# Second feed-forward product: other positions for two row pairs, and weight-block differences made by negated copies and accumulating transfers

## The chip, the cores and the metric

The kernel runs on one core of a Trainium2 chip. The metric is the device time of one execution in microseconds. A core has TensorE (matmuls, from weights loaded into its array and a moving operand), VectorE, ScalarE, GpSimd and SyncE, which here only issues transfers. The engines run side by side and wait for each other by counting semaphores; each works through its own instructions in order.

## The reference, cut to what matters

One layer of a streaming encoder on 256 tokens of width 2048, in float32: a gated convolution and latent attention, a cross attention to 256 memory rows, and a feed-forward of width 8192, which the change is about.

```
def squared_relu_mlp(h, w1, w2):
    return jnp.square(jax.nn.relu(h @ w1)) @ w2
...
x = x + squared_relu_mlp(rms_norm(x, norm_ffn_g[l]), w_ff1[l], w_ff2[l])
```

## The kernel before, in words

**Products in three parts.** A float32 product is made of three matmuls: each factor is split into a high and a low part, and high x high, high x low and low x high are added up (`product`, L2022). The splits of the activations are made once. Those of the weights are made as they stream in: SyncE loads a unit of 128 x 1024 values (two row blocks of 128, each 512 columns wide, 512 KB) into one of four slots of `raw` (`load`, L417); ScalarE copies it to the high part (`hi`, L619); VectorE subtracts that from the raw value for the low part (`lo`, L1075); TensorE uses both. SyncE issues the load of a unit once VectorE has split the unit four before it. ScalarE splits a unit once TensorE has finished the unit four before it. Both run LEAD = 3 units ahead in program order: at step k of a stage ScalarE and VectorE handle unit k + 3.

**The feed-forward.** It is done in four groups (g) of 2048 hidden columns. A group has 32 units of the first product (`still_unit`), and then two half-passes of the second product, p = 0 and 1 (here called pairs of column chunks, or pairs), each 16 units (`seven_pair`, L2027), for output columns 1024p to 1024p + 1023, that is, two chunks c = 0 and 1 of 512. Sixteen row blocks k of the weight times two token blocks t times two chunks are multiplied. For row blocks 0 to 3 the kernel doesn't use the ordinary eight block products of a 2 x 2 by 2 x 2 block matrix but seven (Strassen's scheme in Winograd's form): with A the hidden activations and W the weight, differences and sums of blocks are multiplied. There are two such sides, m = 0 (row blocks 0 and 1) and m = 1 (row blocks 2 and 3).

**Units of a pair.** `FF2_ORDER` lists (c, k) in the order of the units. Twelve are full: two row blocks x two token blocks x three matmuls, 12 matmuls. The unit (0, 2m) is the *left* one of side m, with 6 matmuls, and (1, 2m) the *right* one, with 3; they stand next to each other, at 7 and 8 for m = 0 and at 11 and 12 for m = 1. After the unit at 13 and after the one at 14 come 12 matmuls each on the weight differences of both sides, the tail. That makes 186 matmuls per pair.

**The differences.** While both units of side m stand in `raw`, VectorE's `w_sums` (L1392) makes four differences of their 128 x 512 blocks: t1 = right's first minus left's first and t3 = right's second minus right's first, in one instruction of 1024 elements; t2 = right's second minus t1; t4 = left's second minus t2. It stands ahead of VectorE's split of the left unit, since the slot is loaded anew after that. ScalarE's `ws_high` (L854, steps 5 and 10) copies them to their high parts, VectorE's `ws_low` (L1409, steps 5, 6 and 10, 11) makes the low parts, 1024 elements at a time. Of a right unit only the second half is split for TensorE (`hi_second` L626, `lo_second` L1081).

**The order** on each engine is written out by hand: ScalarE's in its `ff_group` (y_out, then the split of unit k + 3, then ws_high at a step), VectorE's in its own (w_sums, then the split, then ws_low, then the additions of results to the residual), SyncE's in `ff_loads` (L484). GpSimd does nothing in the feed-forward until the last gain vector is loaded. The last pair (g = 3, p = 1) has an order of its own, `LAST_ORDER`, and the output projections and the convolution's (which also use `seven_pair`) keep `FF2_ORDER`.

## Time and profile before

| | us |
|---|---|
| median of 3 runs | 1606.09 (1605.94 to 1606.55) |
| span of the profiled execution, first to last instruction | 1604.8 |
| TensorE busy | 1595.9 (99%) |
| VectorE busy | 1252.5 (78%) |
| ScalarE busy | 866.1 (54%) |
| GpSimd busy | 75.9 (5%) |
| DMA, share of 16 engines, hardware queue | 58.9% |

The profile gives no time of its own for the profiled execution beside the span; the median of the runs stands 1.3 us above it. A matmul's record is longer than the distance to the next one, because they are pipelined: the pace is read from the starts, not from the durations. Engines: PE is TensorE, PEld its weight load, DVE VectorE, ACT ScalarE, POOL GpSimd, SP SyncE; a q behind a name is its issuing side.

### The profile page before, as it was taken

The page shows a single profiled execution, that of the slowest core. Times are in us where ns is not written, and L with a number is a line of the kernel's source. Part 1 is how long each engine was busy: PE and PEld are TensorE (multiplying, and loading weights), DVE is VectorE, ACT ScalarE, POOL GpSimd, SP SyncE. Part 2 cuts the span into 40 slices and gives each one's busy share as a digit, 9 for nine tenths or more (in the row PEclk, how much of TensorE's full clock was granted, in tenths as well). Part 3 has the DMA queues.
Part 4 walks back from the last instruction along what each step waited for, and adds up shares of the span by engine and source line. Part 5 has one row for each costly group of instructions (what it writes and reads, how often), then busy time and mean ns, then how long its engine had stood idle before and what let it go on. Part 6 is the DMA issues. An engine that isn't in the chain of part 4 may idle for free.

```text
span 1604.8 us, 22691 instructions
## 1 busy us (share of the span) xinstructions
PE 1595.9 (99%) x7962; PEld 1352.9 (84%) x7962; DVE 1252.5 (78%) x1681; ACT 866.1 (54%) x1120; POOL 75.9 (5%) x160
## 2 busy tenths in 40 slices
PE   9999999999999999999999999999999999999998
PEld 8888888888888888888888888888888888888886
DVE  5588889999989898786887665885677666866587
ACT  7444456555555556754566655454464455545555
POOL 6500010000000000000000000000000000000001
PEclk9999999999999999999999999999999999999999
DMA  7665645555555665556664566666666666666555
GB/s 256 203 192 184 196 151 171 177 176 174 184 171 170 210 207 181 200 183 238 210 197 138 164 186 191 201 198 190 190 211 196 182 185 196 197 197 187 192 187 182
DMA packets 161294, 304.97 MB, mean 190 GB/s; under 512 B 11689, under 2 KB 20513, under 8 KB 160801
## 3 DMA queue, kind: packets, MB, share of 16 engines
q1 hardware_dynamic: 160128, 300.45, 58.9%
q0 software_dynamic: 1056, 3.46, 0.6%
q8 instruction: 51, 0.84, 0.2%
q14 instruction: 27, 0.22, 0.0%
q10 hardware_dynamic: 32, 0.01, 0.0%
HBM read 301.78 MB, written 2.10 MB: 189 GB/s over the span
## 4 chain that ended last, share of the span: by engine, by line
PE 98%; DVE 1%; DMA 1%; issue 0%; ACT 0%; SPq 0%; ACTq 0%; POOL 0%; DVEq 0%; POOLq 0%
PE ps L2255 15%; PE ps L1750 12%; PE ps L1752 12%; PE ps L1751 12%; PE ps L2025 9%; PE ps L2024 9%; PE ps L2023 9%; PE ps L2257 7%; PE ps L1763 1%; PE ps L1929 1%; PE ps L2146 1%; PE ps L1932 1%; PE ps L1914 1%; PE ps L1913 1%; PE ps L1912 1%; DMA raw<-in_w_ff_dram 1%
## 5 line engine op out<-in xcount | busy, mean ns | idle before, releaser
L1079 DVE TENSOR_TENSOR w_both<-raw,w_both 128x1024 fp32r<-128x1024 f32 x538 | 656.6, 1223 | 257.0 <-ACT w_both L624 255.3
L624 ACT ACTIVATE w_both<-raw 128x1024 fp32r<-128x1024 f32 x538 | 568.7, 1060 | 527.7 <-PE ps L1752 181.7
L2255 PE MATMUL ps<-a_both,w_both 128*128 128x512 f32 x1024 | 321.9, 396 | 0.0
L1750 PE MATMUL ps<-w_both,a_both 128*128 128x512 f32 x636 | 252.4, 397 | 0.1
L1752 PE MATMUL ps<-w_both,a_both 128*128 128x512 f32 x636 | 248.3, 390 | 0.0
L1751 PE MATMUL ps<-w_both,a_both 128*128 128x512 f32 x636 | 248.2, 390 | 0.0
L2257 PEld LDWEIGHTS ps<-a_both,w_both 128*128 128x128 f32 x1024 | 192.5, 188 | 45.2
L1140 DVE SCALAR_TENSOR_TENSOR acc<-hconv,cwk,acc 128x256 f32<-128x256 f32 x464 | 205.1, 497 | 7.4 <-PE ps L1968 7.4
L2257 PE MATMUL ps<-a_both,w_both 128*128 128x256 f32 x1024 | 201.4, 278 | 0.0
L2023 PE MATMUL ps<-w_both,c_hi 128*128 128x512 f32 x504 | 196.7, 390 | 0.3 <-DVE w_both L1079 0.3
L2025 PE MATMUL ps<-w_both,c_lo 128*128 128x512 f32 x504 | 196.4, 390 | 0.0
L2024 PE MATMUL ps<-w_both,c_hi 128*128 128x512 f32 x504 | 196.3, 390 | 0.0
L2255 PEld LDWEIGHTS ps<-a_both,w_both 128*128 128x128 f32 x1024 | 156.3, 189 | 0.3
L1752 PEld LDWEIGHTS ps<-w_both,a_both 128*128 128x128 f32 x636 | 119.5, 188 | 25.1
L1750 PEld LDWEIGHTS ps<-w_both,a_both 128*128 128x128 f32 x636 | 119.6, 188 | 23.8 <-issue 0.3
L1751 PEld LDWEIGHTS ps<-w_both,a_both 128*128 128x128 f32 x636 | 119.7, 188 | 23.3
L2023 PEld LDWEIGHTS ps<-w_both,c_hi 128*128 128x128 f32 x504 | 94.7, 188 | 20.2 <-DVE w_both L1079 0.8
L2025 PEld LDWEIGHTS ps<-w_both,c_lo 128*128 128x128 f32 x504 | 94.7, 188 | 19.4
L2024 PEld LDWEIGHTS ps<-w_both,c_hi 128*128 128x128 f32 x504 | 94.7, 188 | 19.4
L1750 PE MATMUL ps<-w_both,c_hi 128*128 128x512 f32 x128 | 50.2, 392 | 0.0
L1752 PE MATMUL ps<-w_both,c_lo 128*128 128x512 f32 x128 | 49.9, 390 | 0.0
L1751 PE MATMUL ps<-w_both,c_hi 128*128 128x512 f32 x128 | 49.9, 390 | 0.0
(377 smaller groups left out, 1920.3 us busy)
## 6 DMA issues: line engine op xcount, KB each, us to landing
raw<-in_w_ff_dram SPq DMA_DIRECT2D x256, 512.0 KB, 4.1
raw<-in_w_in_dram SPq DMA_DIRECT2D x144, 512.0 KB, 3.6
raw<-in_w_mla_out_dram SPq DMA_DIRECT2D x32, 512.0 KB, 3.7
raw<-in_w_conv_out_dram SPq DMA_DIRECT2D x32, 512.0 KB, 4.3
raw<-in_w_out_dram SPq DMA_DIRECT2D x32, 512.0 KB, 4.5
raw<-in_w_ukv_dram SPq DMA_DIRECT2D x16, 512.0 KB, 3.8
raw<-in_w_xkv_dram SPq DMA_DIRECT2D x16, 512.0 KB, 4.0
raw<-in_w_uq_dram SPq DMA_DIRECT2D x16, 384.0 KB, 3.3
```

The costliest lines, as they stand in the source:

```text
L624: act.activation(whi[:, s, :], raw[:, s, :], ACT.Copy).then_inc(hi_ready, 1)
L1079: dve.tensor_tensor(wlo[:, s, :], raw[:, s, :], whi[:, s, :].bitcast(F32), ALU.subtract).then_inc(lo_ready, 1)
L1140: ins = dve.scalar_tensor_tensor(out=to, in0=h[:, tap:tap + SEQ], scalar=cwk[:, tap:tap + 1], in1=to, op0=ALU.mult, op1=ALU.add)
L1750: pe.matmul(sum_, x_hi[:, k0 + k, tok], w_hi, start=(first and k == 0), stop=False)
L1751: pe.matmul(sum_, x_hi[:, k0 + k, tok], w_lo, start=False, stop=False)
L1752: mm = pe.matmul(sum_, x_lo[:, k0 + k, tok], w_hi, start=False, stop=(last and k == kts - 1))
L1763: tr = pe.transpose(ps[:, first + b, SEQ * (k % 2) + P * t:SEQ * (k % 2) + P * (t + 1)], src[:, t, c0 + P * k:c0 + P * (k + 1)], ident[:])
L2023: pe.matmul(ps[:, bank, :], x_hi, w_hi, start=first, stop=False, skip_group_check=True)
L2024: pe.matmul(ps[:, bank, :], x_hi, w_lo, start=False, stop=False, skip_group_check=True)
L2025: return pe.matmul(ps[:, bank, :], x_lo, w_hi, start=False, stop=last, skip_group_check=True)
L2255: pe.matmul(both, whi[:, s, cols[n]], a_both[:, :, k0 + k, :], start=(first and k == 0), stop=False)
L2257: mm = pe.matmul(ps[:, b0 + b + n, 0:SEQ], wlo[:, s, cols[n]], a_hi[:, k0 + k, :], start=False, stop=(last and k == 1))
```

## The change

In seven of the eight pairs (all but the last):

- the order of the units is `FF_ORDER`: left and right units stand at 6 and 7 (m = 0) and at 9 and 10 (m = 1). The tail stays after the units at 13 and 14.
- `w_sums` is not called. Instead ScalarE's `negated` writes minus the first block of the left unit (step 3 for m = 0, step 6 for m = 1) and minus the first block of the right unit (steps 4 and 7) to the two halves of a buffer t13, ahead of its split of that unit. GpSimd then issues one accumulating transfer, which adds the right unit's two blocks from HBM to t13: that gives t1 and t3.
- SyncE loads the second blocks of the right and the left unit to a buffer t24, by two transfers of 256 KB, behind the loads of units 4 (m = 0) and 7 (m = 1).
- VectorE's `t_sums`, ahead of its splits at steps 6 (m = 0) and 9 (m = 1), waits for both and subtracts twice on 512 elements: t2 and t4, in place.
- ScalarE's `ts_high` (steps 6 and 10) and VectorE's `ts_low` (steps 6, 7 and 10, 11) do for t13 and t24 what `ws_high` and `ws_low` did for `w_sum`.

Context is cut to a line around each edit; a line "..." marks what is left out.

```diff
@@ -140,6 +140,10 @@
 LAST_LEFT, LAST_RIGHT = (3, 8), (4, 9)
+FF_ORDER = ((0, 4), (0, 6), (1, 4), (1, 6), (0, 8), (1, 8), (0, 0), (1, 0), (0, 10), (0, 2),
+            (1, 2), (1, 10), (0, 12), (0, 14), (1, 12), (1, 14))
+FF_LEFT, FF_RIGHT = (6, 9), (7, 10)
+TAIL = 13
 OUT = -1
...
 SEVENS = 2 * GROUPS + 3
@@ -163,6 +167,11 @@
+
+def made_before(g, p):
+
+    return 6 * (p + 1) if g is OUT else g * 8 + (4 * p + 18)
 def turn_pieces(n):
@@ -278,6 +287,8 @@
         ws_lo = ((ws_a0_lo, ws_b0_lo), (ws_a1_lo, ws_b1_lo))
+        t13 = (at(o - nbytes([P, TT, 2 * D]) + 8192, "t13_0", [P, 2 * NC]), at(o + 12288, "t13_1", [P, 2 * NC]))
+        t24 = (at(o - nbytes([P, TT, 2 * D]) + 12288, "t24_0", [P, 2 * NC]), at(o + 2048, "t24_1", [P, 2 * NC]))
         late = Sevens(w_sum, ws_hi, ws_lo, h_sum, h_hi, h_lo, y_copy)
...
         cs_m = [at(o + at_byte, f"cs_m{n}", [P, 2 * NC], F32R) for n, at_byte in enumerate((8192, 12288, 24576, 28672))]
@@ -390,6 +401,8 @@
         ones_copied, ones_added = sem("ones_copied"), sem("ones_added")
+        t24_landed, t13_added = [sem("t24_landed0"), sem("t24_landed1")], [sem("t13_added0"), sem("t13_added1")]
+        t_negated = sem("t_negated")
         fin_act, fin_dve, stored = sem("fin_act"), sem("fin_dve"), sem("stored")
         xq_bank = (2 * pair_of(N_XQ), 4)
@@ -485,9 +498,14 @@
                 for p in range(2):
-                    for i, (c, k) in enumerate(LAST_ORDER if last and p else FF2_ORDER):
+                    for i, (c, k) in enumerate(LAST_ORDER if last and p else FF_ORDER):
                         n = 2 * p + c
                         load(U_FF + UPC * CH + FF2_UNITS * p + i, r, w_ff2[:, ds(g * KT + k, 2), NC * n:NC * (n + 1)])
+                        if i in (4, 7) and not (last and p):
+                            m = (4, 7).index(i)
+                            sp.wait_ge(ws_lo_ready, g * 8 + (4 * p + 12))
+                            sp.dma_start(t24[m][:, 0:NC], w_ff2[:, g * KT + (2 * m + 1), NC * (2 * p + 1):NC * (2 * p + 2)]).then_inc(t24_landed[m], 16)
+                            sp.dma_start(t24[m][:, NC:], w_ff2[:, g * KT + (2 * m + 1), NC * (2 * p):NC * (2 * p + 1)]).then_inc(t24_landed[m], 16)
...
                 ff_loads(g, g * FF_UNITS, False)
@@ -602,6 +620,14 @@
+
+            for n in range(2 * GROUPS - 1):
+                g, p = n // 2, n % 2
+                for m in range(2):
+                    k = g * KT + 2 * m
+                    pool.wait_ge(t_negated, 4 * n + 2 * m + 2)
+                    pool.dma_start(t13[m][:].rearrange("p (k n) -> p k n", k=2), w_ff2[:, k:k + 2, NC * (2 * p + 1):NC * (2 * p + 2)],
+                                   accum_op=ALU.add).then_inc(t13_added[m], 16)
...
             pool.dma_start(fin_g[:], final_norm_g.rearrange("(o n) -> o n", o=1).to_broadcast([P, D])).then_inc(fin_landed, 16)
@@ -853,9 +879,22 @@
-                act.wait_ge(ws_made, g * 12 + (6 * p + 3 * (m + 1) + 18))
+                act.wait_ge(ws_made, made_before(g, p) + 3 * (m + 1))
                 for half in (1, 0):
...
+
+            def negated(g, p, m, u, n, r):
+
+                act.wait_ge(ws_lo_ready, g * 8 + (4 * p + 12))
+                s = u % RING
+                act.wait_ge(landed[s], 16 * (u // RING + 1) + r * (16 // RING))
+                act.activation(t13[m][:, NC * n:NC * (n + 1)], raw[:, s, 0:NC], ACT.Copy, scale=-1.0).then_inc(t_negated, 1)
+
+            def ts_high(g, p, m):
+
+                act.wait_ge(ws_made, g * 8 + (4 * p + 2 * m + 20))
+                for half, t in ((1, t24), (0, t13)):
+                    act.activation(late.ws_hi[m][half][:], t[m][:], ACT.Copy).then_inc(ws_hi_ready, 1)
...
@@ -1024,11 +1063,18 @@
                     ends = last and p == 1
-                    right, sums = (LAST_RIGHT, (1, 7)) if ends else (RIGHT, (5, 10))
+                    right, sums = (LAST_RIGHT, (1, 7)) if ends else (FF_RIGHT, (6, 10))
+                    tail = LAST_LEFT[1] + 2 if ends else TAIL
                     for k in range(FF2_UNITS):
                         n = UPC * CH + FF2_UNITS * p + k + LEAD
-                        if k == right[1]:
+                        if k == tail - 1:
                             y_out(g, p, 0)
+                        if not ends:
+                            for m in range(2):
+                                if k + LEAD == FF_LEFT[m]:
+                                    negated(g, p, m, U_FF + n, 0, r)
+                                if k + LEAD == FF_RIGHT[m]:
+                                    negated(g, p, m, U_FF + n, 1, r)
                         if k + LEAD in right:
...
                         elif not last or n < FF_UNITS:
@@ -1037,9 +1083,11 @@
                             ff_high(CH - 1, g * CH + CH)
-                        if k in sums:
+                        if k in sums and ends:
                             ws_high(g, p, sums.index(k))
-                        if k == right[1] + 2:
+                        elif k in sums:
+                            ts_high(g, p, sums.index(k))
+                        if k == tail + 1:
                             y_out(g, p, 1)
...
                             act.wait_ge(chunk_out, N_END - CH + 2)
@@ -1391,7 +1439,7 @@
-                done = 6 * p + 3 * m + 18
+                done = made_before(g, p) + 3 * m
                 u += left_at[m]
...
                 for n in range(2):
@@ -1401,10 +1449,25 @@
                                   ALU.subtract).then_inc(ws_made, 1)
-                dve.wait_ge(ws_made, g * 12 + (done + 1))
+                dve.wait_ge(ws_made, done + 1)
                 dve.tensor_tensor(t2, right[:, NC:], t1, ALU.subtract).then_inc(ws_made, 1)
-                dve.wait_ge(ws_made, g * 12 + (done + 2))
+                dve.wait_ge(ws_made, done + 2)
                 dve.tensor_tensor(t4, left[:, NC:], t2, ALU.subtract).then_inc(ws_made, 1)
+
+            def t_sums(g, p, m):
+
+                done = g * 8 + (4 * p + 2 * m + 18)
+                dve.wait_ge(t13_added[m], g * 32 + (16 * p + 16))
+                dve.wait_ge(t24_landed[m], g * 64 + (32 * p + 32))
+                dve.tensor_tensor(t24[m][:, 0:NC], t24[m][:, 0:NC], t13[m][:, 0:NC], ALU.subtract).then_inc(ws_made, 1)
+                dve.wait_ge(ws_made, done + 1)
+                dve.tensor_tensor(t24[m][:, NC:], t24[m][:, NC:], t24[m][:, 0:NC], ALU.subtract).then_inc(ws_made, 1)
+
+            def ts_low(g, p, m, half):
+
+                dve.wait_ge(ws_hi_ready, g * 8 + (4 * p + 2 * m + 2 - half + 12))
+                dve.tensor_tensor(late.ws_lo[m][half][:], (t13, t24)[half][m][:], late.ws_hi[m][half][:].bitcast(F32),
+                                  ALU.subtract).then_inc(ws_lo_ready, 1)
...
@@ -1671,14 +1734,17 @@
                     ends = last and p == 1
-                    left, right, lows = (LAST_LEFT, LAST_RIGHT, ((1, 2), (7, 8))) if ends else (LEFT, RIGHT, ((5, 6), (10, 11)))
+                    left, right, lows = (LAST_LEFT, LAST_RIGHT, ((1, 2), (7, 8))) if ends else (FF_LEFT, FF_RIGHT, ((6, 7), (10, 11)))
+                    tail = LAST_LEFT[1] + 2 if ends else TAIL
                     u = UPC * CH + FF2_UNITS * p
...
                         i = k + LEAD
-                        if i in left:
+                        if i in left and ends:
                             w_sums(g, p, left.index(i), U_FF + u, r, left)
+                        if not ends and k in (6, 9):
+                            t_sums(g, p, (6, 9).index(k))
                         if i in right:
...
                         elif not last or u + i < FF_UNITS:
@@ -1689,11 +1755,11 @@
                             if k in lows[m]:
-                                ws_low(g, p, m, 1 - lows[m].index(k))
-                        if k == right[1] + 2:
+                                (ws_low if ends else ts_low)(g, p, m, 1 - lows[m].index(k))
+                        if k == tail + 1:
                             dve.wait_ge(p4_done, g * 2 + (p + 4))
                             add_chunk(p, 0)
-                        if k == right[1] + 3:
+                        if k == tail + 2:
                             add_copies(g, p, g * CH + (N_FF + 2 * p + 1))
...
                             add_last(g, p)
@@ -2024,7 +2090,7 @@
-            def seven_pair(g, p, u, r, banks, first_use, between, sums, b=late, x_hi=c_hi, x_lo=c_lo, order=FF2_ORDER, left=LEFT, right=RIGHT):
+            def seven_pair(g, p, u, r, banks, first_use, between, sums, b=late, x_hi=c_hi, x_lo=c_lo, order=FF2_ORDER, left=LEFT, right=RIGHT, tail=TAIL):
...
                     tok = slice(P * t, P * (t + 1))
@@ -2062,11 +2128,11 @@
                             for t in range(TT):
-                                ends = n == 1 and (i == 15 or (i == left[1] + 2 and t == 0))
+                                ends = n == 1 and (i == 15 or (i == tail and t == 0))
                                 mm = product(banks[c] + t, *hidden(k + n, t), *slot(i, n), first=banks[c] + t not in begun, last=ends)
...
                         mm.then_inc(used, 1)
-                    if i == left[1] + 2:
+                    if i == tail:
                         pe.wait_ge(ws_lo_ready, g * 8 + (4 * p + 15))
...
                         for m in range(2):
@@ -2075,7 +2141,7 @@
                         mm.then_inc(p4_done, 1)
-                    if i == left[1] + 3:
+                    if i == tail + 1:
                         pe.wait_ge(ws_lo_ready, g * 8 + (4 * p + 16))
...
                         for m in range(2):
@@ -2283,18 +2349,19 @@
                     pe.wait_ge(ff_lo, g * CH + (k // 4 + 1))
-                    if i == LEFT[0]:
+                    if i == FF_LEFT[0]:
                         pe.wait_ge(ff_sum, g * CH + CH)
...
-                    if i == (LAST_LEFT if last else LEFT)[0]:
+                    if i == (LAST_LEFT if last else FF_LEFT)[0]:
                         pe.wait_ge(mixed, g * 6 + 12)
                 u = U_FF + UPC * CH
-                seven_pair(g, 0, u, r, FF2_BANKS[0], ff_waits, lambda i: None, g + 3)
+                plain = dict(order=FF_ORDER, left=FF_LEFT, right=FF_RIGHT)
+                seven_pair(g, 0, u, r, FF2_BANKS[0], ff_waits, lambda i: None, g + 3, **plain)
                 pe.wait_ge(chunk_out, g * CH + (N_FF + 1))
-                seven_pair(g, 1, u + FF2_UNITS, r, FF2_BANKS[1], mixed_waits, lambda i: None, g + 3, **dict(order=LAST_ORDER, left=LAST_LEFT, right=LAST_RIGHT) if last else {})
+                seven_pair(g, 1, u + FF2_UNITS, r, FF2_BANKS[1], mixed_waits, lambda i: None, g + 3, **dict(order=LAST_ORDER, left=LAST_LEFT, right=LAST_RIGHT, tail=LAST_LEFT[1] + 2) if last else plain)
...
             for g in range(1, GROUPS - 1):
```

## Rows read from the trace of the kernel before

**Rows 1.** The page: parts 1 to 3, whole execution.
```profile
span 1604.8 us, 22691 instructions
...
PE 1595.9 (99%) x7962; PEld 1352.9 (84%) x7962; DVE 1252.5 (78%) x1681; ACT 866.1 (54%) x1120; POOL 75.9 (5%) x160
...
PEclk9999999999999999999999999999999999999999
...
q1 hardware_dynamic: 160128, 300.45, 58.9%
q0 software_dynamic: 1056, 3.46, 0.6%
```
**Rows 2.** The page, part 4: the chain that ended last, by engine.
```profile
PE 98%; DVE 1%; DMA 1%; issue 0%; ACT 0%; SPq 0%; ACTq 0%; POOL 0%; DVEq 0%; POOLq 0%
```
**Rows 3.** Waits of TensorE: total us, times, longest us.
```profile
PE ps L1779 <- POOL stat L517: 1.5, 1, 1.5
PE ps L2023 <- DVE w_both L1079: 0.3, 1, 0.3
```
**Rows 4.** Windows on the second product's stretches, one per group: busy us by engine.
```profile
992.30:1076.60 84.30, 84.30 (x374) 69.88 (x373) 68.21 (x65) 44.24 (x47) 0.00 (x0) 1.00 0.64 205
...
1339.30:1424.30 85.00, 84.67 (x375) 69.81 (x374) 68.56 (x64) 44.49 (x47) 0.00 (x0) 1.00 0.63 204
```
**Rows 5.** Timeline of ScalarE, group 0, p = 1: start, us, operation [idle before].
```profile
1042.90 1.06 ACT L624 ACTIVATE w_both<-raw 128x1024 fp32r<-128x1024 f32 x1 [1.66 <-PE ps L2025]
1045.62 1.06 ACT L624 ACTIVATE w_both<-raw 128x1024 fp32r<-128x1024 f32 x1 [1.66 <-PE ps L2025]
1048.34 0.63 ACT L631 ACTIVATE w_both<-raw 128x512 fp32r<-128x512 f32 x1 [1.66 <-PE ps L2025]
...
1053.78 1.06 ACT L624 ACTIVATE w_both<-raw 128x1024 fp32r<-128x1024 f32 x1 [1.66 <-PE ps L2025]
1055.14 1.06 ACT L624 ACTIVATE w_both<-raw 128x1024 fp32r<-128x1024 f32 x1 [0.30 <-PE ps L2025]
...
1058.54 1.06 ACT L624 ACTIVATE w_both<-raw 128x1024 fp32r<-128x1024 f32 x1 [1.82 <-PE ps L2025]
1059.51 1.04 ACT L858 ACTIVATE ws_b_hi<-w_sum 128x1024 fp32r<-128x1024 f32 x1
1060.45 1.04 ACT L858 ACTIVATE ws<-w_sum 128x1024 fp32r<-128x1024 f32 x1
1061.40 1.04 ACT L624 ACTIVATE w_both<-raw 128x1024 fp32r<-128x1024 f32 x1
```
**Rows 6.** Timeline of VectorE, the same pair: differences of side 1, then a split.
```profile
1056.02 1.22 DVE L1402 TENSOR_TENSOR w_sum<-raw 128x1024 f32<-128x1024 f32 x1
1057.27 0.69 DVE L1405 TENSOR_TENSOR w_sum<-raw,w_sum 128x512 f32<-128x512 f32 x1
1058.00 0.69 DVE L1407 TENSOR_TENSOR w_sum<-raw,w_sum 128x512 f32<-128x512 f32 x1
1058.61 1.22 DVE L1079 TENSOR_TENSOR w_both<-raw,w_both 128x1024 fp32r<-128x1024 f32 x1
```
**Rows 7.** Waits of VectorE, 992 to 1590 us: total us, times, longest.
```profile
DVE w_both L1079 <- ACT w_both L624: 144.2, 127, 2.4
```
**Rows 8.** Timeline of VectorE around the gap of the third group.
```profile
1362.45 1.23 DVE L1402 TENSOR_TENSOR w_sum<-raw 128x1024 f32<-128x1024 f32 x1 [1.58 <-DMA raw<-in_w_ff_dram]
```
**Rows 9.** SyncE's load line, all calls: ns min/median/max of an issue; to landing.
```profile
L420 SPq DMA_DIRECT2D raw<-in_w_ff_dram x256: 367/373/383, 880.4 to 1576.7; - x128
...
DMA to landing us min/median/max: 3.2/3.9/10.9
```
**Rows 10.** Windows: GpSimd's loads of mem; one pair. Last columns: clock, DMA share, GB/s.
```profile
536.30:572.00 35.70, 35.70 (x167) 29.77 (x166) 32.30 (x57) 23.56 (x34) 3.04 (x4) 1.00 0.71 245
1033.80:1076.60 42.80, 42.80 (x190) 35.50 (x189) 34.00 (x33) 20.66 (x22) 0.00 (x0) 1.00 0.62 201
```
**Rows 11.** The DMA view, issues by line: KB each, median us to landing.
```profile
raw<-in_w_ff_dram SPq DMA_DIRECT2D x256, 512.0 KB, 4.1
...
cw_rows<-in_conv_w_dram POOLq DMA_DIRECT2D x1, 248.0 KB, 3.6
...
vec_rows<-in_q_norm_g_dram POOLq DMA_DIRECT2D x1, 2.0 KB, 2.5
vec_rows<-in_kv_norm_g_dram POOLq DMA_DIRECT2D x1, 2.0 KB, 3.9
```
**Rows 12.** GpSimd's load line for mem, 512 KB each: ns of an issue; to landing.
```profile
L601 POOL DMA_DIRECT2D rows<-in_mem_dram x4: 724/740/842, 536.5 to 565.0; - x4
...
DMA to landing us min/median/max: 4.9/5.7/6.9
```
**Rows 13.** SyncE's load line, 1355.0 to 1356.0 us: two loads and who waited.
```profile
  DVE w_sum L1402: 1.6, 1
...
DMA to landing us min/median/max: 3.8/5.3/6.7
```

## The prediction, made before the change was run

> **What bounds the kernel now.** I read the page first. TensorE is busy for 1595.9 of 1604.8 us, at the full granted clock in every slice, while VectorE stands at 78% and ScalarE at 54% [rows 1]. The chain that ended last is 98% TensorE [rows 2]. Of all waits of TensorE the view of waits finds two, 1.5 us at the start and 0.3 us behind a weight split [rows 3]. So there is next to nothing to gain by relieving another engine: what the change can do is leave TensorE gapless or open gaps in it.
>
> Then the stretches of the feed-forward's second product: two half-passes ("pairs", p = 0 and 1) in each of four groups. A stretch of two pairs takes 84.3 us with TensorE busy throughout; only the third has a gap, 0.3 us [rows 4]. A pair is 12 full units of 12 matmuls, two left units of 6, two right units of 3 and a tail of 24, 186 matmuls, and 372 in the two pairs. Only seven of the eight pairs are changed, and each keeps its 186.
>
> Third, the pace. ScalarE's split of unit k+3 starts when TensorE leaves unit k-1, for the ring has four slots: the copies start at 1042.90, 1045.62, 1048.34, so a full unit takes 2.72 us; 1053.78 to 1055.14 is a left unit, 1.36 us; 1055.14 is the start of the right one, 0.68 us long [rows 5]. One matmul is therefore 0.227 us.
>
> **What it takes off.** On VectorE, of each side of a pair, w_sums' 128x1024 subtraction (1.22 us) goes; the two 128x512 ones (0.69 us each) stay, as t_sums [rows 6]. That is 2.4 us per pair, 17 us in seven. VectorE waited 144.2 us for ScalarE's splits over these groups [rows 7], so the relief lengthens a wait. Worth nothing; at most the 0.3 us gap of the third group goes, where VectorE stood 1.6 us for a late weight load [rows 8].
>
> **What it adds beside other work.** ScalarE: four negated 128x512 copies per pair, 0.63 us each by its own 128x512 split [rows 5], 2.5 us in 42 us of a pair; its copies wait 1.66 us for TensorE at most units [rows 5], so the time as such is free, its place is not (below). SP: four issues of 0.37 us [rows 9] per pair, put behind loads 4 and 7; load 5 waits for the split of unit 1, which is later than that. The wait put ahead of them, for the preceding pair's splits, has been met by step 11 of that pair, while load 4 is issued at its step 13. DMA: a pair loads 16 x 512 KB now, at a share of 0.62 [rows 10]; 4 x 256 KB and 2 x 512 KB come on top, a quarter more, so 0.78, or up to 0.85 if an accumulating byte costs twice. A load is issued when VectorE has split the unit four earlier, some 2.3 us into a full unit, and lands in 4.1 us [rows 11]; it is wanted at the start of the unit three earlier. Behind full units that leaves 10.9 - 2.3 - 4.1 = 4.5 us; before the short units less, but the product itself is three units further on. I put it at nothing, with up to 1 us per pair (7 us) in the range.
>
> **What it puts on the path.** The second side's differences. Follow one pair from T, the moment TensorE begins unit 6 (left of side 0):
> - ScalarE starts the split of unit 9 at T, pitch 0.97 (1058.54 to 1059.51) [rows 5].
> - At the same step 6, in order, come ts_high's two copies, 0.95 each (1059.51, 1060.45, 1061.40) [rows 5]: done issuing at T + 2.9.
> - Step 7 begins with the negated copy of unit 10 (0.6): T + 3.5. It stands behind ts_high because ScalarE works in order; this is what decides.
> - GpSimd may issue the accumulating transfer only now. Call L the time from its issue to the landing: T + 3.5 + L, and 0.1 for the semaphores.
> - VectorE's t_sums at step 9: 0.73 + 0.61 (1057.27, 1058.00, 1058.61) [rows 6]: T + 4.9 + L.
> - Then, behind it in VectorE's order, the split of unit 12, 1.22: T + 6.2 + L with its semaphore.
>
> TensorE wants unit 12 after units 6 to 11: 6+3+12+6+3+12 = 42 matmuls, 9.5 us. So it stands still for **L - 3.3 us** in each changed pair.
>
> Side 0 has more room. Its last negated copy follows the split of unit 6, 1.6 us into unit 3; the transfer lands at 1.6 + L, t_sums end at 3.0 + L after that start. ScalarE wants them for ts_high at 8.16 + 0.97 = 9.1 after it. Up to L = 6.1 nothing happens; beyond, every microsecond also moves ts_high, the copy of unit 10 and all that follows, so the stall grows at twice the rate: (L - 3.3) + (L - 6.1). Queued behind VectorE's wait at step 6 is the split of unit 9, which can bear L = 8.7.
>
> **The unknown, L.** No accumulating transfer is in the trace. GpSimd's own plain loads of the same shape (128 partitions, 2 x 2 KB, 512 KB) took 4.9, 5.7 (median) and 6.9 us from issue to landing [rows 12], beside weight loads at a DMA share of 0.71 [rows 10], between today's share here and the one to come. The largest small one, 248 KB of conv_w, took 3.6 [rows 11]. SP's 512 KB took 4.1 in these groups and 3.2 at the least anywhere [rows 9, 11]. An accumulating transfer reads what it adds to as well. All of queue 1 moved 300.45 MB in 58.9% of 1604.8 us [rows 1], 318 GB/s, so a second pass over 512 KB would be 1.65 us. Ends: 4.9, as the fastest plain one, and 6.9 + 1.65 = 8.5; below 4.9 only by becoming quicker than every plain 512 KB load of this engine. I take 6.5: the median 5.7 with half a second pass.
>
> Sum: stall per pair (6.5 - 3.3) + (6.5 - 6.1) = 3.6 us; seven pairs 25 us; nothing taken back. The span goes from 1604.8 to about 1630. The median of the runs stands 1.3 us above the span: 1631 us.
>
> The Trainium skill speaks the other way. Its page "DMA: Bandwidth & Descriptors", section "Anatomy of one DMA — SWDGE (gpsimd) path", gives such a transfer as about 2.0 us plus bytes over 436 GB/s; for 512 KB that is an estimate of 3.2 us, which would leave no stall at all. The plain loads of this trace [rows 12] disagree by 1.7 to 3.7 us, so I weigh it as the rival below and no more.
>
> **Rivals.**
> - *No stall (not slower).* One mechanism: the accumulating transfer lands within 3.3 us of its issue, so the split of unit 12 is ready at 9.5 us. Then 1606, at best 0.3 below (the gap in group three). Up to L = 3.8 it still reads as no change (7 x 0.45 = 3.2 us). For it: 3.2 us at the least for SP, and 2.5 to 3.9 for GpSimd's small loads [rows 9, 11]. Against: all four 512 KB loads of GpSimd. By the skill's rule just named the trace would have to come out here. 6%, with under 1% for measurably faster.
> - *Quick but late.* L between 3.8 and 4.9: 3 to 11 us, 1610 to 1617. The transfer would have to beat the plain ones. 9%.
> - *Accumulation is slow.* The engines take two or three passes, or its packets queue behind weight loads and delay these too: L = 9 gives (5.7 + 2.9) x 7 = 60 us, 1666, and from 8.7 on unit 9 is late as well. For it: the share rises to 0.78 and more just where units are short, and a load that took 6.7 us to land [rows 13] already made the one gap of this region [rows 8]. Against: queue 0 moved 3.46 MB in 0.6% [rows 1], the same rate as queue 1. 17%.
> - *Forecast*, L from 4.9 to 8.7: 1617 to 1662. 68%.
>
> **The numbers.** Time 1631. Range 1615 to 1664: it leaves out the no-stall case, a part of the quick one, and most of the slow one. What a measurement of this kernel can tell from no change is about 0.2%, 3.2 us. Faster 0.01, within 0.2% 0.06, slower 0.93.
>
> **What would show it.** In the changed trace: the same number of matmuls; the first three stretches of two pairs 91.5 us instead of 84.3, and the fourth, with one changed pair, 3.6 longer. TensorE's waits on VectorE's split (L1079's successor), seven times or more, the largest just before the unit after the second right one. VectorE waiting seven times for the transfer to t13_1, some 3.9 us each (it is at step 9 at T + 6.2, the transfer at T + 3.6 + L), and little or nothing for t13_0. GpSimd's 14 accumulating issues with about 6.5 us to landing. ScalarE's negated copy of unit 10 some 3 us after the split of unit 9 began. If the gaps stand at other units (12's neighbours 9 or 13), the weight loads are what is late; if the waits for t13_1 are there and TensorE shows no gap, the 9.5 us are wrong; if L is below 3.8, the whole forecast is.

## The result and the profile after

The changed kernel takes 1677.8 us (median of 4 runs, 1676.9 to 1680.9) against 1606.0 before: the ratio is 1.045, with a 95% interval of 1.044 to 1.046. That is 72 us slower. The prediction was slower, 1631 us with a range to 1664: the sign was right, the size was not.

The page after, parts 1 to 3, as in [rows 1]:

```profile
span 1679.1 us, 22813 instructions
...
PE 1623.0 (97%) x7962; PEld 1363.5 (81%) x7962; DVE 1237.4 (74%) x1667; ACT 881.2 (52%) x1148; POOL 93.0 (6%) x174
...
q1 hardware_dynamic: 164160, 307.80, 59.2%
q0 software_dynamic: 4864, 10.80, 3.4%
```

TensorE issues the same 7962 matmuls. Its idle time in the span went from 8.9 to 56.1 us (47.2 more), and its busy time rose by 27.1 us: together the 74.3 us of the span. The windows of the four stretches of the second product (of [rows 4]; the columns are busy us by engine, then the granted clock, DMA share and GB/s):

```profile
992.10:1098.50 106.40, 93.69 (x375) 74.30 (x374) 63.95 (x61) 48.22 (x55) 4.85 (x4) 0.92 0.68 199
1187.60:1293.30 105.70, 91.20 (x374) 72.49 (x374) 63.98 (x60) 48.33 (x55) 4.79 (x4) 0.95 0.68 200
1382.40:1487.50 105.10, 92.36 (x375) 73.29 (x374) 63.96 (x60) 48.32 (x55) 4.81 (x4) 0.94 0.69 201
1576.70:1661.20 84.50, 77.48 (x327) 62.59 (x326) 59.77 (x57) 45.33 (x56) 2.99 (x3) 0.96 0.64 194
```

A stretch of two pairs takes 105 to 106 us instead of 84.3, and the one with a single changed pair is 11 us longer. So all the time is in these stretches, some 10.5 us per changed pair, and the granted clock is no longer 1.00 in them. Waits of TensorE (as in [rows 3]), then of VectorE, and GpSimd's accumulating transfers by their line:

```profile
PE ps L2089 <- DVE w_both L1127: 39.9, 21, 4.6
PE ps L2089 <- DVE w_both L1133: 7.1, 7, 1.0
```

```profile
DVE t L1462 <- DMA t<-in_w_ff_dram: 57.1, 14, 5.3
```

```profile
L629 POOL DMA_DIRECT2D t<-in_w_ff_dram x14: 1194/1203/1255, 1002.4 to 1600.6; - x14
...
DMA to landing us min/median/max: 7.0/8.9/10.2
```

Four waits of TensorE per pair (28 in seven), not one; fourteen waits of VectorE for a transfer, both sides; and 8.9 us to landing where 6.5 was assumed. That median mixes two kinds: side 0's seven transfers took 9.3 to 10.2 us, side 1's 7.0 to 8.5. GpSimd spends 1.2 us to issue one, against 0.74 for its plain loads [rows 12]. For the weight loads that SyncE issued between 985 and 1600 us no engine waited; they landed after 3.6, 4.5 (median) and 9.4 us.

One pair (group 1, p = 1) shows the chain. VectorE:

```profile
1261.31 0.69 DVE L1462 TENSOR_TENSOR t<-t,t 128x512 f32<-128x512 f32 x1 [3.82 <-DMA t<-in_w_ff_dram]
...
1265.85 0.69 DVE L1133 TENSOR_TENSOR w_both<-raw,w_both 128x512 fp32r<-128x512 f32 x1 [0.77 <-ACT w_both L657]
...
1272.73 0.69 DVE L1462 TENSOR_TENSOR t<-t,t 128x512 f32<-128x512 f32 x1 [3.92 <-DMA t<-in_w_ff_dram]
```

ScalarE and GpSimd:

```profile
1262.76 2.01 ACT L897 ACTIVATE ws<-t 128x1024 fp32r<-128x1024 f32 x2 [3.81 <-DVE t L1464]
1264.68 0.62 ACT L891 ACTIVATE t<-raw 128x512 f32<-128x512 f32 x1
1265.20 0.61 ACT L657 ACTIVATE w_both<-raw 128x512 fp32r<-128x512 f32 x1
```

```profile
1265.59 1.20 POOL L629 DMA_DIRECT2D t<-in_w_ff_dram  x1 [12.78 <-ACT t L891]
```

Side 0 lands so late that t_sums start at 1261.3; ts_high (L897) waits 3.8 us for them; only then come the negated copy (1264.7) and the split of unit 10 (1265.2); only then GpSimd's second transfer (1265.6), for which VectorE waits 3.9 us more. This holds up ScalarE's splits of units 10 and 11 as well, since they stand behind ts_high: TensorE has gaps of 1.3, 1.0 and 1.3 us ahead of units 9, 10 and 11. The fourth gap, ahead of unit 12, ends like this:

```profile
1275.34 0.79 PE L2089 MATMUL ps<-w_both,c_hi 128*128 128x512 f32 x1 [2.12 <-DVE w_both L1127]
1275.93 0.63 PE L2090 MATMUL ps<-w_both,c_hi 128*128 128x512 f32 x1
1276.36 0.63 PE L2091 MATMUL ps<-w_both,c_lo 128*128 128x512 f32 x1
1276.79 0.63 PE L2089 MATMUL ps<-w_both,c_hi 128*128 128x512 f32 x1
```

The starts are 0.43 us apart (0.59 behind the first) where they were 0.227, and the window on these four has a granted clock of 0.50:

```profile
1275.30:1277.00 1.70, 1.66 (x4) 1.37 (x5) 1.70 (x2) 1.70 (x2) 0.00 (x0) 0.50 0.27 46
```

After these gaps TensorE runs at the lower of its two levels, 1.2 instead of 2.4 GHz.

How late unit 12 is can be read from the starts. In this pair TensorE begins unit 6 here:

```profile
1257.69 0.39 PE L2089 MATMUL ps<-w_both,c_hi 128*128 128x512 f32 x1
```

The 42 matmuls up to unit 12 take 17.6 us instead of 9.5. Of the 8.1 us more, 5.7 are idle time and 2.4 slow matmuls. Over the seven pairs the same count gives 60 us by which unit 12 is late, 47 of them idle and 13 in slow matmuls; another 15 us of slow matmuls stand behind unit 12. Together that is 75 us, and the span grew by 74.

### The profile page after: what moved, and what is told of

It reads as the page before. It is cut to its first block, busy times and chain, and to the rows that moved or that the text cites. A ratio compares the mean times of both kernels' runs of the same rounds, so it can differ in the third digit from the quotient of the medians.

```text
span 1679.1 us, 22813 instructions
## 1 busy us (share of the span) xinstructions
PE 1623.0 (97%) x7962; PEld 1363.5 (81%) x7962; DVE 1237.4 (74%) x1667; ACT 881.2 (52%) x1148; POOL 93.0 (6%) x174
## 3 DMA queue, kind: packets, MB, share of 16 engines
q0 software_dynamic: 4864, 10.80, 3.4%
## 4 chain that ended last, share of the span: by engine, by line
PE 91%; DMA 6%; DVE 1%; ACT 1%; issue 1%; ACTq 0%; POOL 0%; SPq 0%; DVEq 0%; POOLq 0%
PE ps L2321 14%; PE ps L1816 12%; PE ps L1818 12%; PE ps L1817 12%; PE ps L2089 8%; PE ps L2090 7%; PE ps L2091 7%; PE ps L2323 7%; DMA t<-in_w_ff_dram 4%; DMA raw<-in_w_ff_dram 1%; PE ps L1829 1%; PE ps L1995 1%; PE ps L2212 1%; PE ps L1998 1%; DVE w_both L1127 1%
## 5 line engine op out<-in xcount | busy, mean ns | idle before, releaser
L2089 PE MATMUL ps<-w_both,c_hi 128*128 128x512 f32 x504 | 207.8, 412 | 39.9 <-DVE w_both L1127 39.9
L2090 PE MATMUL ps<-w_both,c_hi 128*128 128x512 f32 x504 | 203.7, 404 | 0.0
L2091 PE MATMUL ps<-w_both,c_lo 128*128 128x512 f32 x504 | 203.3, 403 | 0.0
L2089 PEld LDWEIGHTS ps<-w_both,c_hi 128*128 128x128 f32 x504 | 99.6, 198 | 69.4 <-DVE w_both L1127 48.9
L1817 PEld LDWEIGHTS ps<-w_both,a_both 128*128 128x128 f32 x636 | 119.6, 188 | 23.3
L2091 PEld LDWEIGHTS ps<-w_both,c_lo 128*128 128x128 f32 x504 | 99.1, 197 | 22.0
L2090 PEld LDWEIGHTS ps<-w_both,c_hi 128*128 128x128 f32 x504 | 99.8, 198 | 20.4
L629 POOL DMA_DIRECT2D t<-in_w_ff_dram x14 | 16.9, 1204 | 982.9 <-ACT t L891 982.9
L1462 DVE TENSOR_TENSOR t<-t,t 128x512 f32<-128x512 f32 x14 | 9.7, 692 | 57.1 <-DMA t<-in_w_ff_dram 57.1
L1816 PE MATMUL ps<-w_both,c_hi 128*128 128x512 f32 x128 | 50.1, 392 | 0.0
```

The source lines that it names most:

```text
L629: pool.dma_start(t13[m][:].rearrange("p (k n) -> p k n", k=2), w_ff2[:, k:k + 2, NC * (2 * p + 1):NC * (2 * p + 2)], accum_op=ALU.add).the ...
L1816: pe.matmul(sum_, x_hi[:, k0 + k, tok], w_hi, start=(first and k == 0), stop=False)
L1817: pe.matmul(sum_, x_hi[:, k0 + k, tok], w_lo, start=False, stop=False)
L2089: pe.matmul(ps[:, bank, :], x_hi, w_hi, start=first, stop=False, skip_group_check=True)
L2090: pe.matmul(ps[:, bank, :], x_hi, w_lo, start=False, stop=False, skip_group_check=True)
L2091: return pe.matmul(ps[:, bank, :], x_lo, w_hi, start=False, stop=last, skip_group_check=True)
```

## The experiments

Three theories. **A**: the time from issue to landing of the accumulating transfer, in a chain that leads over ScalarE's order, makes the gaps, and the clock that falls behind them adds to it. **B**: the added bytes delay the weight loads, and these make the gaps. **C**: the new positions alone starve the ring.

**1. order_only**: the new positions alone, with differences made by VectorE from the slots.

```diff
-                dve.tensor_tensor(t1_t3..., right..., raw[:, s:s + 2, 0:NC], ALU.subtract).then_inc(ws_made, 1)
+                    dve.tensor_tensor(t1_t3[:, 0:NC], right[:, 0:NC], left[:, 0:NC], ALU.subtract).then_inc(ws_made, 1)
+                    dve.tensor_tensor(t1_t3[:, NC:], right[:, NC:], right[:, 0:NC], ALU.subtract).then_inc(ws_made, 1)
```

> The kernel before with only the new positions: left and right units at 6, 7 and 9, 10; the differences stay VectorE's own subtractions from the weight slots (the first one as two of 512 elements, since the right unit's slot does not always follow the left one's), no negated copies, no added transfers. Theory A (the chain behind the accumulating transfer makes the gaps, and the clock that falls behind them adds to it): nothing of this is here, 1606 us, within 2. Theory B (the added transfers crowd the weight loads): also 1606. Theory C (short units too close together starve the ring of four slots): a good part of the 72 us, at least 1620.

Measured: 1609.5 us, ratio 1.002 (1.001 to 1.003). That is 1.5 us above what A and B expected. C falls: the positions cost 3.3 us, with an instruction more per side on VectorE and with the work on side 0's differences one step earlier on ScalarE and VectorE than before.

**2. ride**: the kernel before, its transfers added, nobody waits.

```diff
+                            sp.dma_start(ride24[:, 0:NC], ...).then_inc(ride24_landed, 16)
+                            sp.dma_start(ride24[:, NC:], ...).then_inc(ride24_landed, 16)
...
+                    pool.wait_ge(hi_ready, U_FF + FF_UNITS * g + UPC * CH + FF2_UNITS * p + (7, 11)[m] + 1)
+                    pool.dma_start(ride13..., w_ff2[...], accum_op=ALU.add).then_inc(ride13_added, 16)
```

> The kernel before, in its own order and with its own subtractions, and beside it all added transfers of the change (per changed pair four of 256 KB from SyncE and two accumulating ones of 512 KB from GpSimd) into buffers that nobody reads. Theory A: the engines wait for none of it, so 1606 to 1609 us. Theory B: the weight loads land later by what the transfers take, gaps stand ahead of the splits, and most of the 72 us appears, at least 1640. The accumulating transfers should take 7 to 10 us here too if their time is their own and not made by the place in the order.

Measured: 1611.1 us (six runs, 1609.5 to 1614.3), ratio 1.003 (1.002 to 1.005), a little above A's figure and far below B's. ScalarE's negated copies are not in this kernel. GpSimd's line in it:

```profile
L625 POOL DMA_DIRECT2D ride<-in_w_ff_dram x14: 1194/1203/1255, 1005.8 to 1538.5; - x14
...
DMA to landing us min/median/max: 6.8/7.2/7.8
```

Even with no engine waiting for it an accumulating transfer takes 7.2 us, where the plain loads of mem took 5.7 [rows 12].

**3. plain**: the changed kernel without `accum_op`.

```diff
-                                   accum_op=ALU.add).then_inc(t13_added[m], 16)
+                                   ).then_inc(t13_added[m], 16)
```

> The changed kernel with GpSimd's transfers to t13 plain instead of accumulating (the addition of the negated copy is left out), same bytes, same waits. Theory A: the stall follows the time L to landing. If a plain transfer takes 5.7 us as the loads of mem did, the idle time is 2.4 us in each of seven pairs, 17 us, and little clock is lost: 1620 to 1628. Theory B and C: bytes and places are the same, so the time stays within 10 us of 1678.

Measured: 1640.3 us, ratio 1.022 (1.020 to 1.024); 5.1, 6.5 and 7.2 us to landing, and VectorE waits 24.6 us for it instead of 57.1. A expected 1620 to 1628, for 5.7 us; with the 6.5 measured the prediction's formula gives 25 us, 1631. The profile shows where the other 9 us are: TensorE's idle time is 23.3 us above that of the kernel before, and its busy time 9.4 us (1605.3 against 1595.9), which is slow matmuls. Accumulation, with what its longer time sets off, is worth 37.5 us of the 72. In the same places in the order a plain transfer takes 6.5 us and an accumulating one 8.9 (medians).

**4. fill**: TensorE is given work in the gaps.

```diff
+                    if order is FF_ORDER and i in FILL:
+                        for _ in range(FILL[i]):
+                            pe.matmul(ps[:, 0 if p else 6, :], c_hi[:, 8, 0:P], c_hi[:, 4:6, :], start=True, stop=True, ...)
                     pe.wait_ge(lo_ready, u + i + 1 + r)
```

> The changed kernel with 29 additional matmuls per changed pair whose result nobody reads (6, 5, 6 and 12 of 512 columns, 0.227 us each), put ahead of TensorE's waits for units 9, 10, 11 and 12, where the profile of the changed kernel has gaps of 1.2 to 1.5 us and of 2.0 to 4.7 us. If the 121 matmuls at a pace of 0.43 instead of 0.227 us come from a clock that falls because TensorE stood idle, the clock stays at 1.0 and the time falls by up to the 22.7 us that they cost: 1655 to 1662 (in some places the added matmuls are longer than the gap). If the clock's fall has another cause, the time stays at 1678 or rises by up to 5.

Measured: 1664.2 us, ratio 1.036 (1.035 to 1.038), 13.6 us faster with 203 matmuls more. TensorE in its page:

```profile
PE 1647.4 (99%) x8165; PEld 1388.0 (84%) x8165; DVE 1237.2 (74%) x1667; ACT 879.8 (53%) x1148; POOL 93.4 (6%) x174
```

203 x 0.227 = 46.1 us of that are the added ones; the others take 1601.3 us, against 1623.0 with gaps and 1595.9 before. The mean granted clock is 0.999 instead of 0.984. So the slow matmuls are a consequence of the idle time, and 22 us of busy time are gone with it. The gain is smaller, since half of the slow matmuls stood ahead of unit 12, where TensorE had to wait for the split anyway; that some added matmuls are longer than their gap can add to this, which the run doesn't show by itself.

**5. neg_early**: the negated copy of the right unit one step earlier, the only edit.

```diff
-                                if k + LEAD == FF_RIGHT[m]:
-                                    negated(g, p, m, U_FF + n, 1, r)
+                                if k + LEAD + 1 == FF_RIGHT[m]:
+                                    negated(g, p, m, U_FF + n + 1, 1, r)
```

> The changed kernel with one edit: ScalarE's negated copy of each right unit stands one step earlier, ahead of the split of units 6 and 9 and so ahead of ts_high of side 0. The weight slot of unit 10 is landed by then. Theory A: the transfer of side 1 starts some 4.5 us earlier relative to TensorE, so with 7.2 to 9.6 us to landing the split of unit 12 is 0 to 2 us late in a pair, and side 0's transfer, also earlier, no longer holds unit 9: idle time 0 to 14 us in all, clock loss under 5, 1609 to 1624. Theory B (the added bytes themselves): stays above 1650. That the accumulating transfer is slow in any place is common to both.

Measured: 1622.8 us, ratio 1.010 (1.009 to 1.012). 55 of the 72 us are gone by moving one copy of 0.6 us per side in ScalarE's order, with every transfer and byte in place. B, as the cause of the 72 us, falls here, as it did with the changed kernel's own trace, in which nobody waits for a weight load.

**6. repaired**: in addition the uses later.

```diff
-                    right, sums = ... else (FF_RIGHT, (6, 10))
+                    right, sums = ... else (FF_RIGHT, (7, 10))
-                        if not ends and k in (6, 9):
+                        if not ends and k in (7, 10):
```

> As the kernel before this one, and t_sums, ts_high and the low parts of side 0 one step later (7 and 7, 8) and t_sums of side 1 one step later (10). Theory A: even 9.6 us to landing is then inside the room that the order gives (side 0 lands before VectorE comes to step 7, side 1 about 8.8 us after unit 6 begins, while the split behind it, of unit 13, is wanted at 12.2), so no gap is left but what the added transfers cost by themselves, 1606 to 1612 us. Theory B: above 1650.

Measured: 1643.9 us, ratio 1.023 (1.022 to 1.025). A miss: 21 us worse than neg_early. VectorE does not wait for the accumulating transfers any more, and TensorE's longest gaps, 2.7 us, stand ahead of unit 11. TensorE is idle for 9.5 us more than in neg_early and busy for 11.2 us more (1611.5 against 1600.3). In ScalarE's order the split of unit 9 stands behind a copy that waits for unit 10's load. That is so in neg_early too, with 20 us of such waits in either. What is new is that t_sums stand behind VectorE's part of that late split, so ts_high has to wait for t_sums, and the split of unit 11 stands behind ts_high:

```profile
1246.28 2.01 ACT L897 ACTIVATE ws<-t 128x1024 fp32r<-128x1024 f32 x2 [2.10 <-DVE t L1464]
```

Three weight loads issued beside side 0's transfer (1232 to 1237 us), and who waited for one:

```profile
  ACT t L891: 2.6, 1
...
DMA to landing us min/median/max: 5.3/6.6/7.1
```

So B holds in a smaller form: beside this accumulating transfer the three loads took 5.3 to 7.1 us, against a median of 4.1 before [rows 11], and an order that leans on one pays.

**7. ts_late**: the negated copies where they were, ts_high of side 0 behind them.

> The changed kernel with ts_high of side 0 one step later (7, behind the negated copy and the split of unit 10), its low parts at 7 and 8; the negated copies and t_sums stay. This takes away the link by which a late side 0 delays side 1's transfer, and 1.9 us of ScalarE's work ahead of it. Theory A: the stall at unit 12 is L - 5.1 (2.1 us at 7.2, 4.5 at 9.6), the one at unit 9 stays at about 1, those at 10 and 11 go: 3 to 5.5 us idle per pair instead of 7.4, and less clock lost: 1635 to 1655. If the link is not what made the gaps at 10 and 11, they stay and the time is within 5 of 1678.

The edit is that of repaired's first two lines and low parts at 7 and 8. Measured: 1632.2 us, ratio 1.016 (1.015 to 1.018), 3 us below the range that A gave. The link from a late side 0 over ts_high to side 1's transfer, with the 1.9 us of ts_high itself that no longer stand ahead of that transfer, is worth 46 us; this run doesn't separate the two. The gap ahead of unit 10 is gone, the one ahead of unit 11 stays, at 0.8 us, against the expectation. Side 1's transfers land in 5.9 to 6.2 us here, side 0's in 9.5 to 10.2.

**8. half**: half the accumulating bytes.

```diff
-                    pool.dma_start(t13[m][:].rearrange("p (k n) -> p k n", k=2), w_ff2[:, k:k + 2, ...],
+                    pool.dma_start(t13[m][:, 0:NC], w_ff2[:, k, ...],
```

> The changed kernel with accumulating transfers of half the size, 256 KB (only the first of the two blocks is added; t3 lacks it). It asks how much of the 7 to 10 us is bytes. If an accumulating byte costs about 1.75 times a plain one (the share of queue 0 per byte in the two profiles), half of them land 1.5 to 2 us sooner, side 1 at about 5.5 and side 0 at 7.5 us, and the time falls by 20 to 30 us. If the time to landing is mostly fixed, it stays within 5 us of 1678.

Measured, in a single run: 1634.2 us; 4.9, 6.3 and 6.9 us to landing. The time falls by 44 us, more than expected, because side 0 drops from some 9.6 to 6.4 us (medians), near the 6.1 up to which the prediction has no doubling.

**9. spread**: the order laid out anew for a side 1 of 6 to 7 us.

> The changed kernel with its waits spread anew: the negated copy of each right unit directly behind ScalarE's split of the left unit (steps 3 and 6; in the run repaired it stood ahead of it and made that split wait for unit 10's landing), t_sums at 7 and 10, ts_high at 8 and 10, low parts at 8, 9 and 10, 11. Theory A: side 0's transfer (9.6 us beside the weight loads) lands 11.2 us after unit 3 begins, just before VectorE's step 7; ts_high of side 0 at step 8 holds neither unit 10 nor unit 11; side 1's (6 to 7 us) lands 8 to 9 us after unit 6 begins, its differences and the split of unit 13 are done by 11.7, wanted at 12.2. What is left is what the run with transfers that nobody reads cost, 3 to 6 us: 1609 to 1614 us, at full clock. If instead the weight loads delayed by side 0's transfer make gaps of their own here, there are idle times ahead of units 9 to 11 in each pair and the time is 1618 or more.

Measured: 1639.0 us, ratio 1.020 (1.017 to 1.024). Another miss. Its accumulating transfers and the two weight loads issued between 1232.9 and 1235.2 us:

```profile
L629 POOL DMA_DIRECT2D t<-in_w_ff_dram x14: 1194/1203/1255, 1003.3 to 1560.5; - x14
...
DMA to landing us min/median/max: 6.4/9.4/10.2
```

```profile
DMA to landing us min/median/max: 8.1/8.3/8.5
```

Side 1 takes 8.5 to 9.4 us in five of the seven pairs, 6.4 and 7.1 in the others. What moves during such a transfer goes with it: spread's side 1 (9.3 us, 1061.9 to 1071.2) and neg_early's (6.1 us, 1190.9 to 1197.1), by queue: packets, MB, share.

```profile
q1 hardware_dynamic: 980, 1.90, 54.8%
q0 software_dynamic: 272, 0.52, 38.4%
```

```profile
q0 software_dynamic: 272, 0.52, 56.8%
q1 hardware_dynamic: 206, 0.41, 17.7%
```

Queue 1 moved 1.7 to 2.0 MB beside the five slow ones of spread, 0.8 and 1.2 MB beside its two quicker ones, and 0.4 to 0.8 MB beside side 1's in neg_early. So the transfer is quick where few weight loads move beside it. That a stall is what thins them out, and that they come back without it, is a reading of these traces that no run shows by itself.

**10. ride_new**: order_only with the transfers of ride, at units 6 and 9.

> The new positions with VectorE's own subtractions (as in order_only, 1609.5 us) and beside them all added transfers into buffers that nobody reads, GpSimd's issued when ScalarE has split units 6 and 9, about where spread and ts_late issue them. It asks what the transfers do to the weight loads in these positions. If weight loads at 7 to 8.5 us to landing (seen in the profile of spread) come from the transfers themselves, they are seen here too, and as VectorE wants unit 10's slot at step 6, gaps of 1 us or more per pair follow: 1615 to 1630, with GpSimd's transfers at 9 us and more, since no stall thins out the loads. If those late loads were a result of spread's own waits, the time is within 4 us of order_only plus what ride cost, 1610 to 1616, and GpSimd's transfers take some 7 us as in ride.

Measured: 1622.4 us, ratio 1.010 (1.008 to 1.012), 12.8 us above order_only. VectorE's wait for weight loads in it:

```profile
DVE w_sum L1439 <- DMA raw<-in_w_ff_dram: 11.7, 7, 2.1
```

That is the price of crowding in the new positions, once in each pair. The expectation of 9 us and more for GpSimd's transfers was wrong (6.0, 7.4, 8.5): side 1's took 6.0 to 7.5 us with 0.5 to 1.0 MB of queue 1 beside them. So an order with small gaps doesn't bring back the 9 us by itself; the traffic at that place does.

**11. spread_half**: spread with half the accumulating bytes, the edit of half.

> The run spread (1639.0 us) with accumulating transfers of half the size, 256 KB (t3 lacks its second block). If its gaps at the tail come from bytes that compete, side 1's transfer taking 9 instead of the 6 to 7 us on which spread was laid out, then half the bytes bring both below 7 us and the gaps nearly close: 1608 to 1616. If spread's order itself is at fault, it stays above 1630.

Measured: 1606.5 us, ratio 1.000 (0.999 to 1.001). No gap is left in the second product; 5.6, 6.5 and 6.8 us to landing. The same order is gap-free at 6.5 us and costs 33 us at 9.4.

**12. half_exact**: t3 by one VectorE addition.

```diff
+                dve.tensor_tensor(t13[m][:, NC:], t13[m][:, NC:], t24[m][:, 0:NC], ALU.add)
                 dve.tensor_tensor(t24[m][:, 0:NC], t24[m][:, 0:NC], t13[m][:, 0:NC], ALU.subtract).then_inc(ws_made, 1)
```

> As spread_half (1606.5 us), made whole: GpSimd's transfer of 256 KB adds right's first block for t1, and t3 is made by one VectorE addition of 512 elements (0.7 us) from the negated copy and the block that SyncE's transfer brought. VectorE's work per side is then three instructions of 512 elements instead of one of 1024 and two of 512 before. Theory A: 1606 to 1609 us, the same as the kernel before; nothing can be gained, since TensorE stays the bound. If the gap-free time of spread_half hung on less than 0.7 us of VectorE's time, gaps of some tenths of a us per pair return: 1609 to 1613.

Measured: 1612.4 us, ratio 1.004 (1.003 to 1.005): TensorE waits for VectorE's split seven times, 4.0 us in all and 0.6 at most, the second case. It is the best whole version with transfers, 65 us faster than the change, and still slower than the kernel before, which needs none.

## Why the prediction was wrong

- **What bounds the kernel**: right. VectorE's relief (15 us less busy) brought nothing; no run went below 1606.
- **The place of the stall**: right. The chain over step 6's ts_high, the copy at step 7, the transfer and step 9's t_sums to the split of unit 12 is what the trace shows; neg_early and ts_late each cut it and gave back 55 and 46 us. It was incomplete: ts_high stands ahead of the splits of units 10 and 11 too, so TensorE waited four times per pair. And the prediction's own sign for late weight loads, gaps at units near 12, would have misled: the gaps at 9 to 11 were there, and no engine waited for a weight load.
- **L, the term that failed, above all for side 0.** It was put at 6.5 for both sides, from the median of plain loads and half a second pass. Side 0's transfers took 9.6 us (median), side 1's 7.2. So side 0's term is 9.6 - 6.1 = 3.5 us per pair where the prediction had 0.4, and side 1's 7.2 - 3.3 = 3.9 where it had 3.2. Two parts were missing. A plain transfer in these places takes 6.5 us, not 5.7, and accumulation adds 2.4 to it, not 0.8 (8.9 against 6.5 in plain, as medians over both sides); GpSimd's issue alone is 0.48 us longer. Side 0's transfer also runs beside more traffic: queue 1, weight loads and at times the change's own 256 KB transfers, moved 1.6 to 1.9 MB in its time, against 0.9 to 1.3 MB beside the transfers of ride, which took 6.8 to 7.8 us. The mem loads, taken as equally crowded by their DMA share, were not a measure of it.
- **The formula.** What it gives is how late the split of unit 12 is, not how long TensorE is idle. With each transfer's own time it gives 54 us for the seven pairs, and the starts of the matmuls give 60. Some of the difference lies in the hand-overs between engines: in the pair shown 4.3 us from the start of t_sums to GpSimd's issue, where the prediction's terms add up to 3.8. The 59 us that the median 8.9 gives for both sides is close to the 60 by luck. So are the 3.9 us of VectorE's wait for side 1 in the pair shown, just as predicted (3.8 to 5.3 us over all pairs): the transfer was issued 7.9 us after unit 6 began, not 3.5, and VectorE came later as well.
- **The clock, left out.** The sum counted idle time only. Behind the gaps TensorE's clock fell to the lower level; the matmuls took 27.1 us more, and with 47 us idle that is the 74 us of the span. Of the slow matmuls 13 us stand ahead of unit 12 and only take the place of idle time; the 15 us behind it are what the prediction's sum lacked. In fill, with the gaps mostly filled, 22 of the 27 are gone and the mean granted clock is 0.999 against 0.984. So of the 75 us counted from the starts the sum had 25; L and the hand-overs are 35 more, the clock 15. The Trainium skill's page "TensorE: Matmul & The Clock Gate", section "Part 1: The HAM clock gate", says that the granted clock is set by how busy the array has recently been; fill agrees.
- **Nothing for crowding, up to 7 us in the range**: too low. Without any wait for the transfers it is 12.8 us in the new positions (ride_new less order_only), and 4.8 in the old ones. In the changed kernel itself nobody waited for a weight load of these stretches, so this term is not a part of its 72 us; it is what the repaired orders met.
- **The rivals.** "Accumulation is slow" came out, at 17% and 1666 us for L = 9; its mechanism, with unit 9 late as well, is what the trace shows, except that nobody waited for the weight loads. Its 60 us are what unit 12 is late by; the clock is the rest. "No stall" fell. So did the rule of the Trainium skill's page "DMA: Bandwidth & Descriptors", section "Anatomy of one DMA — SWDGE (gpsimd) path", by which 512 KB would take 3.2 us, as an estimate: every 512 KB transfer of GpSimd took 4.9 us or more.
- **What stays open**: why ride's transfers cost 4.8 us in all while ride_new's cost 12.8. VectorE waits seven times for a weight load in both, 9.0 us in ride and 11.7 in ride_new, but TensorE waits 1.0 us for its splits in ride and 11.6 in ride_new: the old order has the room. No run moved the transfers alone between the two. Also open is why an accumulating transfer slows down as it does beside weight loads; the runs show only that the two go together.

## What to carry to other kernels

In a chain of waits that crosses three engines and a DMA, the time to landing must be priced for each transfer beside the traffic at its own place, and that traffic can change when a stall goes: side 1's transfer took 6 us in neg_early and mostly about 9 in spread. Look for the small instruction that releases the transfer and for what stands ahead of it in its engine's order: here 0.6 us in the wrong place cost 55. And where TensorE is otherwise never idle, a gap costs more than its length: slow matmuls ahead of the next late unit are hidden in the wait for it, those behind the last one are not.

## What the hardware showed that was not expected

- An accumulating transfer of 512 KB is cut into more packets than a plain one of the same shape: queue 0 had 1056 packets before, 4864 after and 3072 in plain, so 272 against 144 for each of the 14. Its share per byte is higher: queue 0 took 3.4% of 16 engines over 1679.1 us, against 2.3% over 1637.5 us in plain. Less the 0.6% of 1604.8 us for its other transfers [rows 1], that is an estimated 47 against 28 us for the 14.
- GpSimd's issue takes 1.2 us for 512 KB accumulating, 0.86 us for 256 KB accumulating and 0.72 us for 512 KB plain.
- Extra matmuls with no use made the kernel 13.6 us faster, by keeping the clock at its upper level.
